# S5's scan result turned back as four products that PE sums

## The reference

```python
bu_re = jnp.einsum('blgc,gpc->blgp', uf, bb_re)
bu_im = jnp.einsum('blgc,gpc->blgp', uf, bb_im)
# h_t = a * h_{t-1} + bu_t, with a = ab_re + i ab_im, |a| = mag
_, _, h_re, h_im = lax.associative_scan(combine, (a_re, a_im, bu_re, bu_im), axis=1)
y = (jnp.einsum('blgp,gcp->blgc', h_re, c_re) - jnp.einsum('blgp,gcp->blgc', h_im, c_im))
y = y + uf * d_skip
y = jax.nn.gelu(y)
y = y * jax.nn.sigmoid(y @ w_glu)
```

## Time and profile before

| | |
|---|---|
| median of 3 runs | 1651.99 us (1650.25 to 1655.81) |
| the profiled execution | 1652.19 us, span 1651.0 us |
| mean granted TensorE clock | 0.944 of full |
| busy share PE / PEld / DVE / ACT / POOL | 90% / 70% / 63% / 46% / 7% |
| where S5's four steps lie | 96.8 to 227.4 us of the span |

### The profile page before, as it was taken

The page is one execution under the profiler, slowest core; times in us unless marked ns, Lnnn a source line. Parts: engine busy times, 40 slices in busy tenths (PEclk is TensorE's granted clock), DMA queues, the critical chain, the costliest instruction groups (busy, mean ns, idle before and its releaser), DMA issues.

```text
span 1651.0 us, 17477 instructions
## 1 busy us (share of the span) xinstructions
PE 1485.6 (90%) x6875; PEld 1163.2 (70%) x6875; DVE 1034.1 (63%) x1359; ACT 756.0 (46%) x994; POOL 121.3 (7%) x143
## 2 busy tenths in 40 slices
PE   6999859989978999999999999999988699999981
PEld 5776548768656788788878788786547578888861
DVE  4889775455324555445545658846444688988876
ACT  5453334644323322222223543244445578788763
POOL 1500000000000000000000203200000011111012
PEclk8999869989999999999999999999999799999996
DMA  5222122202201332232222231210003599999974
GB/s 208 77 77 77 51 77 99 81 26 102 74 28 52 117 150 93 80 135 77 94 70 91 91 102 52 77 52 26 26 1 129 218 369 408 412 411 405 418 298 178
DMA packets 39329, 231.57 MB, mean 140 GB/s; under 512 B 4400, under 2 KB 5696, under 8 KB 17104
## 3 DMA queue, kind: packets, MB, share of 16 engines
q1 hardware_dynamic: 30640, 200.09, 32.3%
q0 software_dynamic: 7648, 27.87, 4.6%
q10 hardware_dynamic: 960, 2.49, 0.4%
HBM read 213.66 MB, written 16.78 MB: 140 GB/s over the span
## 4 chain that ended last, share of the span: by engine, by line
PE 75%; DVE 13%; ACT 6%; issue 4%; DMA 2%; POOL 0%; POOLq 0%; ACTq 0%; DVEq 0%
PE bank L415 14%; PE bank L416 14%; PE bank L417 14%; PE bank L2910 5%; PE bank L2912 5%; PE bank L2911 5%; PE bank L561 3%; DVE w_lo L371 2%; PE bank L434 1%; PE bank L2161 1%; PE bank L2190 1%; PE bank L435 1%; PE bank L436 1%; DVE xbc L926 1%; DVE bu L859 1%
## 5 line engine op out<-in xcount | busy, mean ns | idle before, releaser
L415 PE MATMUL bank<-h_hi,w_hi 128*128 128x512 f32 x952 | 391.1, 411 | 24.6 <-DVE h_lo L495 13.6
L416 PE MATMUL bank<-h_lo,w_hi 128*128 128x512 f32 x952 | 381.1, 400 | 0.0
L417 PE MATMUL bank<-h_hi,w_lo 128*128 128x512 f32 x952 | 380.5, 400 | 0.0
L371 DVE TENSOR_TENSOR w_lo<-w_raw,w_hi 128x2048 fp32r<-128x2048 f32 (+3 forms) x89 | 196.5, 2208 | 92.0 <-ACT w_hi L365 91.4
L415 PEld LDWEIGHTS bank<-h_hi,w_hi 128*128 128x128 f32 x952 | 183.1, 192 | 79.7 <-issue 17.2
L417 PEld LDWEIGHTS bank<-h_hi,w_lo 128*128 128x128 f32 x952 | 182.9, 192 | 43.1
L416 PEld LDWEIGHTS bank<-h_lo,w_hi 128*128 128x128 f32 x952 | 183.3, 193 | 41.5 <-issue 1.9
L365 ACT ACTIVATE w_hi<-w_raw 128x2048 fp32r<-128x2048 f32 (+3 forms) x89 | 158.3, 1779 | 59.9 <-PE bank L417 59.9
L3090 DVE TENSOR_TENSOR h_lo<-w_raw,h_hi 128x2048 fp32r<-128x2048 f32 x32 | 73.2, 2291 | 15.4 <-ACT h_hi L2991 15.4
L3090 DVE TENSOR_TENSOR lo_b<-raw_b,hi_b 128x2048 fp32r<-128x2048 f32 x32 | 73.2, 2288 | 8.8 <-ACT hi_b L2991 8.8
L415 PE MATMUL bank<-a_hi,w_hi 128*128 128x512 f32 x176 | 69.6, 396 | 4.5 <-DVE a_lo L1602 4.5
(11 more groups left out here) (575 smaller groups left out, 2811.1 us busy)
## 6 DMA issues: line engine op xcount, KB each, us to landing
w_raw<-in_params_dram SPq DMA_DIRECT2D x122, 1024.0 KB, 4.9
raw_b<-in_params_dram SPq DMA_DIRECT2D x51, 1024.0 KB, 8.5
w_raw<-in_params_dram SPq DMA_DIRECT2D x16, 704.0 KB, 4.0
result_rows<-osb POOLq DMA_DIRECT2D x16, 512.0 KB, 8.3
result_rows<-prm POOLq DMA_DIRECT2D x8, 512.0 KB, 3.1
xt<-in_x_t_dram POOLq DMA_DIRECT2D x1, 2048.0 KB, 9.3
scratch_rows<-htm SPq DMA_DIRECT2D x4, 512.0 KB, 3.0
out_dram<-pr SPq DMA_DIRECT2D x4, 512.0 KB, 2.6
```

Source lines behind the costliest of these rows:

```text
L371: V.tensor_tensor(k.w_lo[:, g % SPLIT, 0:size], k.raw[:, g % RAW, 0:size], k.w_hi[:, g % SPLIT, 0:size].bitcast(F32), ALU.subtract).then_i ...
L415: PE.matmul(ps, wh, hi[:, c, 0:width], start=c == 0, stop=False)
L416: PE.matmul(ps, wh, lo[:, c, 0:width], start=False, stop=False)
L417: m = PE.matmul(ps, wl, hi[:, c, 0:width], start=False, stop=c == parts - 1)
```

## The change

Turning back is (with `h'` the scan's result) `h_re = b0*ec - b1*es` and `h_im = b1*ec + b0*es`, and then `y = C_re h_re + (-C_im) h_im`. Before, DVE makes four products, one difference and one sum and PE two products with C. Now DVE makes the four products alone, each into a buffer of its own (`gg[0]`, `gg[1]`, `tmp`, and the last one over `bu[0]`), each signalling `s5_rot`; PE multiplies them by `C_re`, `-C_re`, `-C_im` and `-C_im` and accumulates all four in the bank. A step has eight matmuls in `pe_s5_out` in place of four, with a wait of its own before each pair, and the two tiles take turns within it. `-C_re` (`ncb`, 128x256) is made once by DVE, at the end of `dve_s5_matrices`, over the columns of `s5_br` and `s5_bi`, which nobody reads any more. The counts of `s5_rot` become fourfold, and one wait of DVE at the start of a step goes, since `s5_c` covers it.

```diff
@@ -234,6 +234,7 @@
         self.S, self.xdt, self.btm = m("S", [P, TT - 1, SSD_W]), m("xdt", [P, TT, SSD_W]), m("btm", [P, TT, T])
         self.cbt = self.xbc[:, 6:10, :].rearrange("p g (t l) -> p g t l", t=TT)
         a = COLS["s5_br"][0]
+        self.ncb = self.prm[:, a:a + 256].rearrange("p (j c) -> p j c", j=8)
         self.afm = self.prm[0:SSD_H, a:a + T]
         self.sq0 = self.xbc[:, 0:DB, :]
 
@@ -719,6 +720,13 @@
             else:
                 v(m)
 
+    v.own()
+    v(V.memset(k.ncb, 0.0))
+    v.own()
+    for g2 in range(2):
+        r0, c0 = 64 * g2, 16 * g2
+        v(V.tensor_scalar(k.ncb[r0:r0 + 64, :, c0:c0 + 16], cr[r0:r0 + 64, :, :], -1.0, None, ALU.mult))
+
 
 def dve_s5_bt(k):
     V, s = k.nc.vector, k.s
@@ -740,6 +748,7 @@
     for n in range(4):
         h = n % 2
         pe_turn(k, k.bank[4 + n][:, 0:P], bd[:, n // 2, 4 * h:4 * h + 4, :].rearrange("p t c -> p (t c)")).then_inc(s.s5_turn, 1)
+
 
 
 
@@ -797,13 +806,14 @@
 def pe_s5_out(k, q):
     PE, s = k.nc.tensor, k.s
     y = k.bank[6 + q // 2]
-    PE.wait_ge(s.s5_rot, q + 1)
     if q == 2:
         PE.wait_ge(s.m_rs, 1)
-    for jj in range(2):
-        r0 = 32 * ((2 * q + jj) % 4)
-        PE.matmul(y[r0:r0 + 32, :], k.cb[:, 0, 2 * q + jj, :], k.gg[:, 0, jj, :], start=True, stop=False, tile_position=(0, r0))
-        m = PE.matmul(y[r0:r0 + 32, :], k.cb[:, 1, 2 * q + jj, :], k.gg[:, 1, jj, :], start=False, stop=True, tile_position=(0, r0))
+    for n, (c, x) in enumerate(((k.cb[:, 0], k.gg[:, 0]), (k.ncb, k.gg[:, 1]), (k.cb[:, 1], k.tmp), (k.cb[:, 1], k.bu[:, 0]))):
+        PE.wait_ge(s.s5_rot, 4 * q + n + 1)
+        for jj in range(2):
+            r0 = 32 * ((2 * q + jj) % 4)
+            m = PE.matmul(y[r0:r0 + 32, :], c[:, 2 * q + jj, :], x[:, jj, :], start=n == 0, stop=n == 3, tile_position=(0, r0),
+                          skip_group_check=True)
     m.then_inc(s.s5_c, 1)
 
 
@@ -812,7 +822,7 @@
     for n in range(4):
         A.wait_ge(s.s5_bu, 4 * q + n + 1)
         if n == 0 and q > 0:
-            A.wait_ge(s.s5_rot, q)
+            A.wait_ge(s.s5_rot, 4 * q)
         A.activation(k.bu[:, n % 2, n // 2, :], k.bank[4 + n % 2][:, :], ACT.Copy).then_inc(s.s5_buc, 1)
 
 
@@ -828,7 +838,6 @@
     v.own()
     if q > 0:
         V.wait_ge(s.s5_c, q)
-        V.wait_ge(s.s5_rot, q)
     v(V.tensor_tensor(g_[0], b_[0], ec, ALU.mult))
     v(V.tensor_tensor(tmp, b_[1], es, ALU.mult))
     v(V.tensor_tensor(g_[1], b_[1], ec, ALU.mult))
@@ -859,16 +868,12 @@
                 v(V.tensor_tensor_scan(bu[part][:, jj, at], mag, gg[part][:, jj, at], first, ALU.mult, ALU.add))
         yield
     v.own()
-    v(V.tensor_tensor(g_[0], b_[0], ec, ALU.mult))
-    v(V.tensor_tensor(tmp, b_[1], es, ALU.mult))
-    v(V.tensor_tensor(g_[1], b_[1], ec, ALU.mult))
+    V.tensor_tensor(g_[0], b_[0], ec, ALU.mult).then_inc(s.s5_rot, 1)
+    V.tensor_tensor(g_[1], b_[1], es, ALU.mult).then_inc(s.s5_rot, 1)
     yield
-    v.own()
-    v(V.tensor_tensor(g_[0], g_[0], tmp, ALU.subtract))
-    v.own()
-    v(V.tensor_tensor(tmp, b_[0], es, ALU.mult))
-    v.own()
-    V.tensor_tensor(g_[1], g_[1], tmp, ALU.add).then_inc(s.s5_rot, 1)
+    V.tensor_tensor(tmp, b_[1], ec, ALU.mult).then_inc(s.s5_rot, 1)
+    V.wait_ge(s.s5_rot, 4 * q + 1)
+    V.tensor_tensor(b_[0], b_[0], es, ALU.mult).then_inc(s.s5_rot, 1)
 
 
 def dve_s5_skip(k, h):
```

## The result

The changed kernel takes a median of 1643.83 us (1642.87 to 1644.89, 6 runs) beside 1652.37 us (1650.25 to 1657.6, 6 runs) of the kernel before: a ratio of 0.9949, interval 0.9934 to 0.9965. That is 8.5 us or 0.5% faster. It is the number of the rival "the clock holds" (1644.3). The profiled execution took 1644.47 us.

A forecast was written before the change was run, and what follows sets the result against it. PE was taken to bound the kernel mostly, DVE only late in S5. Setup, added matmuls, clock and DVE's saving summed to +0.7 us (A) or -4.7 (B); the middle, -2.0 from 1652.2, gave 1650.2 us, range 1644.5 to 1655.0.

The forecast's parts named there:

- the clock holds: Rival: PE's clock never falls in S5's turns 2 and 3; -7.9 us, 1644.3 us; chance 0.12.
- DVE's saving: Turning back in each S5 step takes DVE 4.7 us for 7.2: 2.5 us a step, 10 us in all.
- turns 2 and 3: S5's outs 0 and 1 with the following `pe_s5_in`: DVE's saving hidden; shift reaches +5.1 us by A, +1.5 by B.
- last step: S5's bare step 3: first product there sooner, eight matmuls take 7.1 us at half clock, PE late next; 2.55 us earlier.
- Setup: DVE's one memset and two scalings for `-C_re`, once, on the chain: +0.75 us, bounds 0.44 and 0.92.
- Tiles side by side: In `pe_s5_out` both column tiles' matmuls overlap, so eight take 3.7 us at full clock, 7.1 at half.
- PE's clock: Term deciding the sign: the clock falls to half each turn, during `pe_s5_in`; when it falls was left open between A and B.
- the middle: Midway between A and B for the whole sum, as no row decided between them: -2.0 us.
- A: Clock falls 5.4 us after the last wide matmul; `pe_s5_in` takes 6.0 us; +0.7 us in all.
- B: Clock falls 3.5 us after `pe_s5_out` ends; `pe_s5_in` takes 4.2 us; -4.7 us in all.
- turn 4: S5's out 2 and last `pe_s5_in`, where PE idled 3.98 us: its end shifts +3.2 us by A, -2.2 by B.
- The change doesn't do what it says: Rival: the last step's matmuls don't start before DVE ends; +1.6 us, 1653.8 us; chance 0.05.

The follow-up runs named there:

- PE kept busy: Changed kernel with the early `w_lo` split and `-C_re` built in step 0, plus 16 unused matmuls before the last out: 1643.73 us, 0.9946.
- a0: The changed kernel run again unaltered, its second execution, as yardstick: 1644.94 us, 0.9955 of the kernel before.
- a1: The changed kernel run again unaltered, its third execution, as yardstick: 1644.00 us, 0.9951 of the kernel before.
- c0: The kernel before, unaltered, profiled a second time: 1651.47 us.
- c1: The kernel before, unaltered, profiled a third time: 1651.41 us.
- the table moved: Changed kernel with DVE's `w_lo` split ahead of the first scans and `-C_re` built in S5's step 0, not the setup: 1644.59 us, 0.9946.
- PE's half alone: Kernel before, with the four matmuls of each of the first three S5 outputs done twice, DVE unchanged: 1655.78 us, 1.0011.
- `w_lo` alone early: Changed kernel with DVE's weight split for the slot behind `z` put ahead of the first half of the scans: 1647.45 us, 0.9960.

## What of the prediction was right, and which step failed

**DVE's saving: right.** 4.55 us for the predicted 4.7, hidden in turns 2 and 3, open in the last step. PE's last wait went from 21.03 to 14.98 us (14.97 or 14.98 in every variant with the new DVE code, the one with PE kept busy aside), and stayed at 21.01 in the one without: 6.05 us, the "some 6" of the prediction.

**Setup: right on DVE, too small on PE.** From the start of the last operation shown ahead of the new ones to the first tap DVE takes 1.15 us for 0.26: 0.89, predicted 0.75. PE's first `pe_s5_in` starts 2.1 us later (98.89 for 96.81), but single executions of one kernel differ by nearly as much: 96.81, 98.39 and 97.97 before, 98.89, 98.66 and 98.16 after. Over all traces the six executions without the table in the setup start it at 96.65 to 98.39, mean 97.3, the eight with it at 97.75 to 99.64, mean 98.8. So the table costs PE some 1.6 us, about twice the predicted term. How much of it is the clock was not tried; it is at half up to 81.3, 81.4 and 79.4 in the three executions of the changed kernel and up to 78.4, 81.1 and 80.6 in those of before.

**Tiles side by side, `pe_s5_out` 3.7 us: right** (3.55), and for the reason given, though the order without alternation shows that it isn't free of the order. There the Trainium skill (TensorE: Matmul & The Clock Gate, Part 3, The mechanism) has matmuls start and end strictly in program order: in the other order of the tiles the fifth matmul of the program (tile 1's first) starts at 131.72, before the fourth (tile 0's last, 132.57), so the trace disagrees. Nor are the tiles quite independent of each other, for then that order too would take 3.55 us.

**The clock: the step that failed.** Under "PE's clock" the prediction had two readings of when the clock falls and took the middle, −2.0 us. Both put the fall within `pe_s5_in`, which was to take 6.0 us by A and 4.2 by B. Measured are 3.79 to 3.80 us in eight of the nine turns of the three executions of the changed kernel, and 4.13 in the ninth (a0, turn 2). Reading A is what failed: it let the new matmuls do nothing to the fall. Where the changed kernel's clock falls at all in turns 2 to 4, it falls 3.3 to 4.4 us after the out's end (a0, a1) and 6.9 to 8.0 after the last wide matmul, which is near B's interval (3.5) and not A's (5.4). By the sum's own terms, against the trace of before:

| us | A | B | middle | measured |
|---|---|---|---|---|
| setup | +0.75 | +0.75 | +0.75 | +1.7 |
| turns 2 and 3 | +4.35 | +0.75 | +2.55 | −1.0 |
| turn 4 | −1.9 | −3.7 | −2.8 | −4.2 |
| last step | −2.55 | −2.55 | −2.55 | −4.3 |
| S5's end | +0.7 | −4.7 | −2.0 | −7.8 |

Of the 5.8 us between the middle and the result, 5 lie in turns 2 to 4, 1.8 in the last step, and the setup takes 1 back. In turn 4 the idle 3.98 us are gone and the second pair takes 1.9 us for 3.78, because it now runs ahead of the fall; B had the first whole and the second nearly. In turns 2 and 3 part of the miss is the base: the forecast was made on an execution in which these two turns took 1.9 us longer than in c0 and c1. There the clock fell 4.9 to 5.1 us after the out's end, where the prediction's three intervals were 2.7 to 4.8, so that neither of its two intervals holds from one execution to the next.

The evidence that the prediction set against "the clock holds" was the fall at 133.0 with PE busy. But what PE did there was the 32-row matmuls of `pe_s5_in`; it was no evidence on matmuls of 128 rows. The run on 32 rows comes near A's world (`pe_s5_in` of 5.6 us for A's 6.0) and ends at +1.0 us, where A's sum was +0.7; between it and the changed kernel lie 8.8 us. The Trainium skill (TensorE: Matmul & The Clock Gate, Why this matters for your kernels) says the clock stays up as long as there are no long idle gaps. The first execution of the changed kernel agrees; a1 doesn't agree, with the clock at half at 138 and PE 1.00 busy, nor does the run on 32 rows: half clock at 139 with PE 1.00 busy.

**The last step: right mechanism, a size off.** The first product was there 6.05 us earlier relative to the end of `pe_s5_in`, as worked out, and PE is late next, as said. But eight matmuls took 5.3 us and not 7.1, because the clock rose at 217.8 in the middle of them: −4.3 for −2.55. It rose at 219.4 in a1, whose last out takes 6.2 us, and at 214.9 where the step began at 211.84 (the table moved; 5.1 us), so this term is good to about 1 us either way. The short step of before was over in 3.56 us, all of it at half clock.

**"The clock holds" had the number by luck.** Its end, −7.9, is the measured −7.8, but its terms aren't: it had −1.5 at the third out (measured +0.7), −5.4 at the end of `pe_s5_in` (−3.5) and −2.55 for the last step (−4.3), and the errors cancel. It had the wait for `w_lo` that caps what the clock is worth in turns 2 and 3. But a0 and a1, in which the clock falls there, end within 0.7 us of the first execution. What decides is turn 4 and the last step, which have no `z` slot and no slack of DVE.

**"The change doesn't do what it says": wrong.** The last out starts at 214.27, when only the first product (212.99 + 1.23) is done.

Open stays what happens behind S5. Between S5's end and the kernel's, single executions drift by −2.1 to +4.2 us against the first trace of before (PE's half alone +4.2, the table moved +3.4, a1 −1.9), in stages that the edits don't touch; what sets this off wasn't tried. The time that the half clock costs behind 240 us (half of its length) goes the same way in these, 60.1, 59.9 and 53.3 us for 56.7 in the trace of before, but not in the one with `w_lo` alone early, 61.6 with a drift of +0.7. Open is also how much of a matmul's size the clock answers to, its rows, its columns or the tile's form.

## What to carry to other kernels

Work taken from a late engine and given to PE can cost less than its duration, if it fills gaps of PE: 5.2 us of added matmuls moved S5's end by −0.8 to +0.6 us. Look where the late engine carries the path, for the gain is made there: all of this one lies in one turn and the bare step behind it. When a chain of wide matmuls is broken by small ones, ask what the clock does in between, and cost the case that it holds and the case that it falls; a fall seen during one shape is no evidence on another. Take a second and a third execution of the kernel before ahead of the forecast: here the first alone was off by 1 to 2 us in single stages, as much as the terms of the sum. Independent tiles of a matmul group go in turn in the program, not one tile after the other.

## What the runs showed of the hardware

- Eight f32 matmuls of 128x32 over 512 columns in two column tiles take 3.55 us in turn and 5.3 us tile by tile, at full clock.
- The same matmuls on 32 rows take the same 3.56 us, but the clock was at half from 135.1 to 145.3 with PE busy throughout; with 128 rows it stayed at full through turns 2 to 4 in one of three executions, and fell later and for shorter in the others (a0: 136.0 to 139.4; a1: 137.5 to 140.9).
- Sixteen matmuls without use ahead of a bare step bring its 5.1 us down to 3.55. They ended 1.1 us after the step's data were there, and no gain in the median could be measured.
- Executions of one kernel differ in when the clock falls: in the kernel before at 133.0, 135.7 and 135.2 in turn 2, for 6.8, 3.4 and 3.4 us.
